# Turning the attention probabilities one half chunk later in two of six phases of a mixer

## The reference

```
h = rmsnorm(x, norm_mix[l])
qa, ka, va, qb, kb, vb, qc, kc, vc, gate_logits = split(h @ w_in[l])     # 1024 -> 5632 columns
y_a = attention with rmsnorm and rope on q and k, softmax over 256 keys
y_b = windowed attention with bias and a sink in the softmax
y_c = differential attention: p[0] - lam * p[1], then values, then a per-head rmsnorm
merged = sum over branches of sigmoid(gate) * (y @ w_branch)
x = x + merged @ w_out[l]
```

## Time and profile before

| | before |
|---|---|
| median of three runs | 2904.37 us |
| the profiled execution | 2901.04 us |
| its span | 2899.1 us |
| PE busy | 2644.0 us (91%) |
| DVE busy | 1399.3 us (48%) |
| ACT busy | 981.5 us (34%) |
| POOL busy | 188.1 us (6%) |

### The profile page before, as it was taken

The page is one execution under the profiler, slowest core; times in us unless marked ns, Lnnn a source line. Parts: engine busy times, 40 slices in busy tenths (PEclk is TensorE's granted clock), DMA queues, the critical chain, the costliest instruction groups (busy, mean ns, idle before and its releaser), DMA issues.

```text
span 2899.1 us, 55899 instructions
## 1 busy us (share of the span) xinstructions
PE 2644.0 (91%) x23862; PEld 1748.5 (60%) x23862; DVE 1399.3 (48%) x2042; ACT 981.5 (34%) x1705; POOL 188.1 (6%) x195
## 2 busy tenths in 40 slices
PE   8999999999999999999999989899999989766676
PEld 6877777878877778875433333344788865332332
DVE  6776767877867767543110001424777763000001
ACT  4435655444446645431100100212455542000000
POOL 0102000000002000000000000002243310000000
PEclk9999999999999999999999999999899999987877
DMA  8764345766763348544899999713000017999998
GB/s 306 276 256 174 121 146 224 297 261 252 300 230 137 139 165 308 215 150 167 352 422 420 422 421 421 304 66 115 17 17 11 11 45 286 421 421 421 421 420 337
DMA packets 103994, 716.95 MB, mean 247 GB/s; under 512 B 11948, under 2 KB 14380, under 8 KB 19800
## 3 DMA queue, kind: packets, MB, share of 16 engines
q1 hardware_dynamic: 93016, 663.75, 57.9%
q10 hardware_dynamic: 10752, 49.81, 4.5%
HBM read 711.65 MB, written 1.86 MB: 246 GB/s over the span
## 4 chain that ended last, share of the span: by engine, by line
PE 62%; DMA 20%; DVE 12%; ACT 3%; issue 2%; SPq 0%; ACTq 0%; DVEq 0%
DMA weight_ring<-in_stream 20%; PE banks L2168 9%; PE banks L668 6%; PE banks L670 6%; PE banks L669 6%; PE banks L1109 3%; PE banks L1998 3%; PE banks L1111 3%; PE banks L1110 3%; PE banks L2533 3%; PE banks L2577 2%; PE banks L2973 1%; PE banks L2059 1%; DVE split_high L1486 1%; DVE split_high L665 1%
## 5 line engine op out<-in xcount | busy, mean ns | idle before, releaser
L2168 PE MATMUL banks<-weight_ring,scratch 128*32 128x256 f32 (+1 forms) x4256 | 557.3, 505 | 147.0 <-DMA weight_ring<-in_stream 145.5
L2168 PEld LDWEIGHTS banks<-weight_ring,scratch 128*32 128x32 f32 (+1 forms) x4256 | 184.0, 129 | 500.4 <-DMA weight_ring<-in_stream 256.6
L665 DVE TENSOR_TENSOR split_high<-weight_ring,split_high 128x1024 fp32r<-128x1024 f32 x198 | 242.8, 1238 | 124.1 <-ACT split_high L660 121.9
L660 ACT CAST split_high<-weight_ring 128x1024 fp32r<-128x1024 f32 x198 | 206.8, 1052 | 273.3 <-PE banks L670 198.5
L2319 DVE TENSOR_TENSOR scratch<-scratch,banks 128x512 f32<-128x512 f32 (+1 forms) x32 | 17.7, 555 | 558.8 <-PE banks L2168 558.8
L1486 DVE TENSOR_TENSOR split_high<-weight_ring,split_high 128x1024 fp32r<-128x1024 f32 x128 | 161.3, 1271 | 115.6 <-ACT split_high L1368 115.5
L668 PE MATMUL banks<-split_high,features_low 128*128 128x512 f32 x480 | 189.9, 396 | 0.2 <-DVE resid L701 0.2
L670 PE MATMUL banks<-split_high,features_high 128*128 128x512 f32 x480 | 187.1, 390 | 0.0
L669 PE MATMUL banks<-split_high,features_high 128*128 128x512 f32 x480 | 186.8, 389 | 0.0
L1368 ACT CAST split_high<-weight_ring 128x1024 fp32r<-128x1024 f32 x128 | 133.5, 1052 | 137.7 <-PE banks L1111 131.9
L2228 ACT ACTIVATE scratch<-banks 128x512 f32<-128x512 f32 (+1 forms) x32 | 15.7, 490 | 469.0 <-PE banks L2168 469.0
(11 more groups left out here) (454 smaller groups left out, 4846.4 us busy)
## 6 DMA issues: line engine op xcount, KB each, us to landing
weight_ring<-in_stream SPq DMA_DIRECT2D x628, 1024.0 KB, 9.8
scratch<-in_kept ACTq DMA_DIRECT2D x24, 1024.0 KB, 8.5
scratch<-in_pair_rows ACTq DMA_DIRECT2D x8, 448.0 KB, 3.6
scratch<-in_kept ACTq DMA_DIRECT2D x6, 512.0 KB, 5.6
scratch<-in_lora ACTq DMA_DIRECT2D x2, 1536.0 KB, 8.9
front<-in_gain_rows ACTq DMA_DIRECT2D x5, 512.0 KB, 4.0
bias<-bias_rows SPq DMA_DIRECT2D x1, 2304.0 KB
scratch<-in_routing ACTq DMA_DIRECT2D x1, 1040.5 KB, 5.0
```

The costliest lines, as they stand in the source:

```text
L660: act.copy(split[i % 4][0], source(i)).then_inc(*self.rounded.up())
L665: dve.tensor_tensor(lo, source(i), hi.bitcast(F32), ALU.subtract).then_inc(*self.rest.up())
L2168: last = pe.matmul(self.psum[q * M:(q + 1) * M, (GATE, UP, DOWN)[part], 0:W], left, w[j][:, q * W:(q + 1) * W], start=(k == 0), stop=(k == ...
```

## The change

In phases 1 and 5 the probabilities are turned at half chunk 23 instead of 22 and 47 instead of 46, and the values follow one half chunk later, at 24 instead of 23 and 48 instead of 47. Both layers run this code, so it happens four times. The number of instructions of each kind stays the same.

```
-        at_scores, at_probs, at_values = (12, 18, 25, 30, 36, 42), (16, 22, 28, 33, 40, 46), (17, 23, 29, 34, 41, 47)
+        at_scores, at_probs, at_values = (12, 18, 25, 30, 36, 42), (16, 23, 28, 33, 40, 47), (17, 24, 29, 34, 41, 48)
```

## The result

| | before | after |
|---|---|---|
| median of the runs | 2903.49 us (6 runs) | 2925.59 us (6 runs) |
| the profiled execution | 2901.04 us | 2925.16 us |
| its span | 2899.1 us | 2923.3 us |

The ratio is 1.0077, 95% interval 1.0064 to 1.009. One of the six runs before took 3057.24 us; it counts as a slow run and the ratio leaves it out, and the median of the other five is 2902.62 us. The forecast was 2921.6 us with a range of 2911 to 2929 us.

The account below looks back on a forecast made before the run. PE's instruction order was taken to bound the mixers. Two layers of 4.6 us (phase 1 and keys) plus 1.75 us (phase 5) gave 12.7 us, with the clock 17.2 us: 2921.6 us, range 2911 to 2929 us.

Parts of the forecast that it names:

- The order on DVE: Phases 1 and 5: DVE makes rests 22 and 46 behind norm_probs, so PE's wait moves earlier and does not go.
- (1): Phase 1: half chunk 22 starts as before after one wait of 3.19 us; 8 transposes follow uncovered, 0.8 us.
- (2): Phase 5: half chunk 46 starts as before after a 4.3 us wait; 16 transposes follow uncovered, 1.75 us.
- (3): Key transposes, phase 1: PE waits 3.8 us for DVE's copy of the values; keys 4.6 us late, 0.8 from (1).
- (4): PE's clock after longer waits: three new drops of about 1.5 us, 4.5 us in all; bounds 0 to 8 us.
- The sum: Both layers: 2 x 6.35 = 12.7 us, with the clock 17.2 us; profiled execution 2918.2 us, median 2921.6 us.
- R1: Rival: rests 22 and 46 ready before the normed probabilities, waits vanish; 12.5 us faster, 2892 us; chance 0.05.
- R2: Rival: only the transposes lose cover, copy of the values comes in time; 5.1 us, 2909.5 to 2911; chance 0.09.
- R3: Rival: the forecast sum without any new clock drop; 2917 us; chance 0.10.
- R4: Rival: no difference, what PE loses is given back later in the kernel; chance 0.04.

Follow-up runs that it names:

- the rests first: Against the changed kernel: DVE makes rests 22 and 46 before norm_probs, ACT rounds both before the exponentials; 2902.09 us, ratio to before 1.0000.
- the kernel kept busy: Against the changed kernel: unused identity transposes put into PE's waits ahead of half chunks 22, 46 and the key transposes; 2913.55 us, ratio to before 1.0025.
- phase 5 alone: Against the kernel before: only phase 5 moved later, to 47 and 48, phase 1 as before; 2908.81 us, ratio 1.0019.

## Why the prediction was right

**The order on DVE.** The point on which all hung, that the rests of 22 and 46 stand behind `norm_probs`, holds: the releaser of both waits is line 1486, and moving the rests, with the roundings that they need, takes away all of them but 0.51 us at 46 (the rests first).

**(1) The transposes of phase 1:** 0.8 us forecast, 0.79 measured in layer 0. **(2) Phase 5:** wait 4.3 us forecast, 4.19 measured. The merged rows begin at 441.28 us in their second half (433.49 before), 7.79 us late, where half chunk 46 was 5.98 us late: 1.81 us for the transposes against 1.75 forecast.

**(3) The keys:** a wait of 3.8 us forecast, 3.88 measured; the keys late by 4.6, measured 4.89 us. The 0.3 us are in the first link: ACT's copies end 0.9 us behind the transposes (302.53 against 301.62), not 0.6, since both groups are now ready at nearly the same time and are copied one behind the other. The table loads are 1.28 us each and the next operation follows at once, here again twice (302.56 to 303.85 and 305.02 to 306.32); the drain of some 1.38 us that the Trainium skill adds (ScalarE: Activation LUTs, "What ACT_TABLE_LOAD costs") does not show in this kernel. By it the keys would have come an estimated 2.8 us later still in each layer, 22.7 us in all; that this total is nearer to the measured one than my 17.2 is chance, since the rows have no such gap.

**(4) The clock** was mis-sized. Right was where the new drops came: after the keys in both layers and at 22 in layer 1, and none new at 22 in layer 0 or at 46. I took 1.5 us for each of three, 4.5 us, and nothing for a drop that was there already. Measured: 1.65 us in layer 0 and 1.56 in layer 1 behind the keys, but 2.40 us for half chunk 22 in layer 1 (5.29 against 2.89), and 1.0 us more at 46 in layer 1 (5.28 us, against 4.32 us from 1014.77 to 1019.09 before). That is 5.6 us for the three and 6.6 us in all. The rows of before held drops of 1.6 us only, and I took them for the price. The price is not fixed: in layer 1 the longer single waits came with drops over a whole half chunk, in layer 0 they did not (22 took 4.45 us after 4.46 before, 46 took 4.44 after 4.54).

**The sum:** 17.2 us forecast, 20.6 measured from the first mixer to line 1762 (20.1 and the 0.53 by which this execution was ahead): 6.6 for the clock against 4.5, and 14.0 for the rest against 12.7. Of this 1.3 us, 0.6 are the handoffs of (3) twice, and 0.6 are the transposes behind 22 and 46 in layer 1, which began at the low clock (1.22 us from start to start against 0.79 in layer 0, and 1.81 against 1.67). They belong to the clock too, and the sum had nothing for them. By the medians the whole change is 22.1 us.

**The rivals.** R1 fell: the waits for probabilities went, but those for rests took their place; made true by an edit, its condition brings the time back to that of before, not to 2892 us. R1 had left out the wait ahead of the keys, 3.1 us in each layer even then. R2 fell by the 3.9 us at line 1236. R3 fell by the windows, and the kernel kept busy prices all drops, the three old ones among them, at 12 to 15 us. R4 fell: the loss stays to the end, as the same 20 us at line 1762 and 24 at the end of the span.

Left open: why the kernel with the rests first, 4.9 us ahead at line 1762 in its profile, shows none of it in its medians; whether the stretch behind depends on where in time it begins; and what decides whether a wait is followed by a drop.

## What to carry to other kernels
- Before moving a step later on one engine to give another engine time, look at which of that other engine's operations the inserted work itself needs. If it stands behind the operation that was waited for, the wait only moves, and whatever ran inside it is uncovered.
- A unit of work that is moved also leaves its old place: ask what it covered there. Here a half chunk no longer stood between the values and the keys, and PE waited 3.9 us for a chain of copies, two table loads, two roundings, a rest and a copy on ACT and DVE; that cost more than the 0.8 us of transposes.
- A wait of 3 to 4 us on PE costs the wait and, in the changed kernel, 1.6 to 2.4 us more by the clock; with the rests first, waits of 3.1 us cost nothing more. Transposes of no use in the waits bought 12 to 15 us back; a better order was worth more.

## What the runs showed of the hardware
- The same wait gave different drops: half chunk 22 took 4.45 us after a wait of 3.20 us in layer 0, and 5.29 us after 3.22 us in layer 1. Waits of 3.09 and 3.10 us ahead of the keys had no drop behind them (the rests first), one of 2.43 us at 46 had one. The length of the wait alone doesn't tell.
- The drop is not the same in every kernel whose code is the same there: half chunk 22 took 4.46 us in layer 0 before the change, and 2.86 us behind nearly the same three waits (1.11, 0.34 and 0.48 us) in the kernel with phase 5 alone.
- With transposes of 128x128 (28 in 3.22 us, 34 in 3.87 us) in the waits, half chunks 22 and 24 in layer 0 had a granted clock of 1.00, 2.4 GHz; in the changed kernel, with nothing in the waits, half chunk 22 had 0.62 and the first 2.80 us of 24 had 0.70.
- A rest on DVE took 2.90 us beside POOL's multiplication of 2.33 us (304.52 to 306.85), against 1.2 us otherwise; before the change it was the same, 2.90 us from 299.56, beside POOL's operation from 299.04.
